# Output products, norm and routing of a one-core encoder layer, joined into one block, with hand-placed memory for the experts' weights

## The reference, cut to what matters

```python
mix = (jax.nn.sigmoid(ga) * ya + jax.nn.sigmoid(gb) * yb) @ w_out[l]
x = layer_norm(ALPHA * x + mix, ln1_g[l], ln1_b[l])
# moe_ffn(x):
scores = jax.nn.sigmoid((xt @ router_w).astype(jnp.float32))        # 512 x 64
_, sel = lax.top_k(scores + router_bias.astype(jnp.float32), TOP_K)  # 6 of 64
wsel = jnp.take_along_axis(scores, sel, axis=-1)
wsel = wsel / jnp.sum(wsel, axis=-1, keepdims=True) * ROUTED_SCALE
# each expert e, on the tokens that chose it:
gu = x_pad[tok] @ w_gate_up[e]                        # 1024 x 512
h = jax.nn.silu(gu[:, :EXPERT_DIM]) * gu[:, EXPERT_DIM:]
return (h @ w_down[e]) * wt[:, None]                  # 256 x 1024
# routed + shared expert, then the second layer_norm
```

## Time and profile before

| | us |
|---|---|
| median of 3 runs (1533.08 to 1539.72) | 1537.55 |
| the profiled execution's own time | 1532.44 |
| its span | 1530.5 |
| mean granted TensorE clock, share of full | 0.926 |

### The profile page before, as it was taken

The page is one execution under the profiler, slowest core; times in us unless marked ns, Lnnn a source line. Parts: engine busy times, 40 slices in busy tenths (PEclk is TensorE's granted clock), DMA queues, the critical chain, the costliest instruction groups (busy, mean ns, idle before and its releaser), DMA issues. The chain is left out here.

```text
span 1530.5 us, 22988 instructions
## 1 busy us (share of the span) xinstructions
PE 1309.1 (86%) x8117; PEld 772.0 (50%) x8118; DVE 444.5 (29%) x876; ACT 302.1 (20%) x817; POOL 290.5 (19%) x353
## 2 busy tenths in 40 slices
PE   6999999999998969999958789979697868978690
PEld 5465555655553438887435335534354434534340
DVE  1545544445416433332226121101010101100015
ACT  1231333223312332222030001111011101111020
POOL 2201111011107010000110222323132312322122
PEclk8999999999998989999977899989798978989795
DMA  4531111113002122334029389999999996899874
GB/s 113 155 115 48 48 41 50 49 44 137 1 1 55 28 76 80 97 96 173 14 88 373 102 305 332 335 393 392 396 371 384 392 383 223 320 374 390 330 228 170
DMA packets 134582, 294.85 MB, mean 193 GB/s; under 512 B 12928, under 2 KB 82688, under 8 KB 117968
## 3 DMA queue, kind: packets, MB, share of 16 engines
q1 hardware_dynamic: 118096, 266.77, 46.6%
q0 software_dynamic: 15552, 25.46, 7.0%
q10 hardware_dynamic: 832, 1.11, 0.2%
HBM read 278.57 MB, written 27.04 MB: 200 GB/s over the span
## 5 line engine op out<-in xcount | busy, mean ns | idle before, releaser
L1724 PE MATMUL bank<-expert_gu,gathered_xT 128*64 128x256 f32 x2048 | 254.0, 404 | 80.7 <-issue 55.5
L1724 PEld LDWEIGHTS bank<-expert_gu,gathered_xT 128*64 128x64 f32 x2048 | 166.7, 146 | 156.9 <-issue 82.9
L423 PE MATMUL bank<-xT,w_head 128*128 128x512 f32 x480 | 241.0, 613 | 1.2 <-PEq L81 1.2
L1872 DVE SCALAR_TENSOR_TENSOR hidden<-gate,slot_w,bank 128x128 f32<-128x128 f32 x64 | 22.2, 347 | 444.6 <-ACT gate L1838 433.1
L1731 PE MATMUL bank<-expert_down,hiddenT 128*64 128x512 f32 x512 | 124.0, 605 | 0.7 <-issue 0.6
L1642 POOL DMA_INDIRECT sum_rows<-expert_y,row_col x64 | 101.3, 1583 | 50.5 <-POOL row_col L1637 47.1
L423 PEld LDWEIGHTS bank<-xT,w_head 128*128 128x128 f32 x480 | 78.8, 190 | 48.5 <-issue 42.4
L1838 ACT ACTIVATE gate<-bank 128x128 f32<-128x128 f32 x64 | 17.8, 277 | 340.6 <-PE bank L1724 335.7
L601 POOL TENSOR_TENSOR LO<-LT_diagonal,level_blocks 128x256 f32<-128x256 f32 x48 | 38.2, 827 | 233.1 <-DVE LT_corner L767 233.1
L1637 POOL COPY row_col<-row_idx 128x1 int32 (+1 forms) x64 | 12.2, 191 | 304.1 <-ACT expert_y L1844 293.1
L1245 DVE TENSOR_TENSOR w_lo<-w_tile,w_hi 128x1024 fp32r<-128x1024 f32 (+1 forms) x32 | 35.5, 1112 | 116.2 <-ACT w_hi L1190 116.2
(11 more groups left out here) (325 smaller groups left out, 1873.0 us busy)
## 6 DMA issues: line engine op xcount, KB each, us to landing
expert_gu<-in_expert_w_gate_up_dram SPq DMA_DIRECT2D x128, 1024.0 KB
expert_down<-in_expert_w_down_dram SPq DMA_DIRECT2D x64, 1024.0 KB
w_head<-in_w_in_dram SPq DMA_DIRECT2D x32, 512.0 KB, 3.7
w_tile<-in_w_in_dram SPq DMA_DIRECT2D x16, 512.0 KB, 3.8
sum_rows<-zero_rows SPq DMA_DIRECT2D x2, 2048.0 KB, 11.8
w_tile<-in_w_branch_a_dram SPq DMA_DIRECT2D x8, 512.0 KB, 5.1
w_pair<-in_w_in_dram SPq DMA_DIRECT2D x6, 512.0 KB, 3.7
x_rows<-in_x_dram SPq DMA_DIRECT2D x4, 512.0 KB
```

The costliest lines, as they stand in the source:

```text
L423: mm = nc.tensor.matmul(bank[:, :], w_head[:, g, c, :], xT[:, c, :], start=(c == 0), stop=(c == KC - 1))
L1724: mm = nc.tensor.matmul(bank[parts[a], 0:2 * P], x[:, c, part], halves[:, a, :, :], start=(c == 0), stop=(c == KC - 1))
```

## The change

The phases `merge_phase` and `route_phase` become one, `mix_phase`, without the barrier between them. What it does:

- TensorE's order: the output products of tile t are interrupted by the transposes of tile t-1 (`turn_x1`) and its logits (`logits`). The transposes read `x_rows` itself with a stride of 8 elements. The shared expert's products are cut to 96 steps (32 of 128 columns, 32 of 256, 32 of 128) and dealt out by `fill(n)` where TensorE would stand.
- The norm takes two VectorE instructions per tile for scaling, gain and offset, and none on GpSimd. VectorE makes the choices of tile t-1 before it normalises tile t.
- Memory: the experts' first weights go where the split inputs (`xh`, `xl`, `dnh`, `dnl`, `w_hi`, `w_lo`, `aoh`, `aol`) lay, and are loaded as soon as the last product that reads these is made. `wo_low` goes to `dnl`, so its load waits too.
- GpSimd issues the gathers of the first four pairs at the end of `mix_phase`, after `idx_ready`; before, they stood at the head of `experts_phase`. The shared expert's down weights are loaded at the head of `experts_phase` by ScalarE's queue, and `shared_down(0)` waits for them.
- The slot of a token's rank in its expert's list changes: `spread` takes the place of `iota_e` in one comparison. Slot 16h + 4l + r holds rank 4h + l + 16((r - h) mod 4). Ranks 0 to 47 filled slots 0 to 47; now they fill three of every four adjacent slots.

```diff
-def merge_phase(nc, mem, T, ps, w_in, w_a, w_b, w_out, ln_g, ln_b, x1_rows):
+def mix_phase(nc, mem, T, ps, w_in, w_a, w_b, w_out, ln_g, ln_b, x1_rows, router_w, router_bias, ws_gu):
...
-    wo_low, wo_high = xT[:, :, :].rearrange("p (c a) n -> p c (a n)", a=2), T["bias"][:, :, :].rearrange("p (c a) n -> p c (a n)", a=2)
+    wo_low, wo_high = (at(f"w_out_{n}", [P, KC // 2, D], n) for n in ("dnl", "bias"))
...
+    x_cols = [T["av"][:, 2 * t:2 * t + 2, :].rearrange("p a n -> p (a n)") for t in range(2)]
...
-            for c, part in ((0, wo_low), (KC // 2, wo_high)):
-                sp.dma_start(part, w_out[c * P:(c + KC // 2) * P, :].rearrange("(c p) n -> p c n", p=P)).then_inc(wo_in, 16)
+            load_out(wo_high, KC // 2)
             sp.wait_ge(ao_split, 1)
...
-            for t in range(TT):
-                sp.wait_ge(permuted[t], 1)
-                sp.dma_start(x1_rows[t * P:(t + 1) * P, :], x_cols[t]).then_inc(x1_out, 16)
-            sp.wait_ge(x1_out, 16 * TT)
+            sp.dma_start(wr[:, :, :], router_w.rearrange("(p c) n -> p c n", p=P)).then_inc(r_in, 16)
+            sp.dma_start(brow[:, :], router_bias.partition_broadcast(P)).then_inc(r_in, 16)
+            sp.wait_ge(prod[1][1], TURNS)
+            load_out(wo_low, 0)
+            T["load_gu"](sp, 2, 2)
+            sp.wait_ge(prod[1][2], TURNS)
+            T["load_gu"](sp, 0, 0)
+            T["load_gu"](sp, 1, 1)
+            sp.wait_ge(prod[1][3], TURNS)
+            for s in range(GROUP):
+                T["load_down"](sp, s, s)
+            sp.dma_start(wg[:, :, :], ws_gu.rearrange("(p c) n -> p c n", p=P)).then_inc(s_in, 16)
+            for t in range(TT - 1):
+                x1_rows_out(t)
+            sp.wait_ge(mix_psum[TT - 1], 1)
+            T["load_gu"](sp, 3, 3)
+            x1_rows_out(TT - 1)
...
+            def mix(t, half, cs):
+                for c in cs:
+                    mm = nc.tensor.matmul(ps[2 * t + half][:, :], mT[:, c, tile(t)], wo(c)[:, half * HALF:(half + 1) * HALF],
+                                          start=(c == 0), stop=(c == KC - 1))
+                return mm
+            def turn_x1(t):
+                pe.wait_ge(ln_done[t], 1)
+                columns = xs[:, t, :].rearrange("p (q c) -> p c q", c=KC)
+                for half in range(2):
+                    for c in range(KC // 2):
+                        mm = nc.tensor.transpose(ps[2 * t + half][:, tile(c)], columns[:, half * KC // 2 + c, :], ident[:, :])
+                    mm.then_inc(x1t_psum[t], 1)
+            def logits(t):
+                pe.wait_ge(x1t_ready[t], 2)
+                for c in range(KC):
+                    mm = nc.tensor.matmul(ps[2 * t][:, 0:NE], xT[:, c, tile(t)], wr[:, c, :], start=(c == 0), stop=(c == KC - 1))
+                mm.then_inc(lg_psum[t], 1)
+            def shared_steps():
+                for lo, hi in ((0, P), (P, 3 * P), (3 * P, SEQ)):
+                    for g in range(4):
+                        for c in range(KC):
+                            mm = nc.tensor.matmul(shared_bank[g][:, lo:hi], wg[:, c, tile(g)], xT[:, c, lo:hi],
+                                                  start=(c == 0), stop=(c == KC - 1))
+                            if hi == SEQ and c == KC - 1:
+                                mm.then_inc(sg_psum[g], 1)
+                            yield
...
             pe.wait_ge(wo_in, 32)
             for p in range(2):
                 pe.wait_ge(merged[p], TURNS)
+            pe.wait_ge(r_in, 32)
             for t in range(TT):
-                for half in range(2):
-                    for c in range(KC):
-                        mm = nc.tensor.matmul(ps[2 * t + half][:, :], mT[:, c, t * P:(t + 1) * P],
-                                              wo(c)[:, half * HALF:(half + 1) * HALF], start=(c == 0), stop=(c == KC - 1))
-                mm.then_inc(mix_psum[t], 1)
-            for c in range(KC):
-                for t in range(TT):
-                    if c == 0:
-                        pe.wait_ge(permuted[t], 1)
-                    if c >= 4:
-                        pe.wait_ge(x1t_ready, c - 3)
-                    mm = nc.tensor.transpose(ps[c % 4][:, t * P:(t + 1) * P], x_cols[t][:, c * P:(c + 1) * P], ident[:, :])
-                mm.then_inc(x1t_psum, 1)
+                mix(t, 0, range(KC))
+                if t:
+                    turn_x1(t - 1)
+                mm = mix(t, 1, range(KC // 2))
+                if t:
+                    logits(t - 1)
+                mix(t, 1, range(KC // 2, KC)).then_inc(mix_psum[t], 1)
+            pe.wait_ge(s_in, 16)
+            pe.wait_ge(sc_done[0], 1)
+            fill(32)
+            turn_x1(TT - 1)
+            fill(3)
+            logits(TT - 1)
+            fill(6)
...
+            fill(23)
+            for part in range(PARTS):
+                pe.wait_ge(lists_ready[part], 1)
...
+                if part < PARTS - 1:
+                    fill(4)
+            mm.then_inc(list_psum, 1)
+            fill(3)
...
+            fill(96)
...
+            for p in range(2):
+                act.wait_ge(merged[p], TURNS)
             for t in range(TT):
+                nc.scalar.preload_act_table_set(LN_EXP)
                 act.wait_ge(ag_done[t], 1)
...
-                if t:
-                    permute(t - 1)
+                nc.scalar.preload_act_table_set(SIGMOID)
+                if t < TT - 1:
+                    permute(t)
+                for half in range(2 if t < TT - 1 else 1):
+                    copy_x1(t, half)
+                act.wait_ge(lg_psum[t], 1)
+                nc.scalar.activation(score[:, t, :], ps[2 * t][:, 0:NE], ACT.Sigmoid).then_inc(sc_done[t], 1)
             permute(TT - 1)
-            for c in range(KC):
-                act.wait_ge(x1t_psum, c + 1)
-                nc.scalar.copy(xT[:, c, :], ps[c % 4][:, :]).then_inc(x1t_ready, 1)
+            nc.scalar.preload_act_table_set(SILU)
+            for k in range(2):
+                act.wait_ge(sg_psum[k], 1)
+                nc.scalar.activation(hT[:, k, :], shared_bank[k][:, :], ACT.Silu).then_inc(sg_act[k], 1)
+                if k == 0:
+                    act.wait_ge(slot_psum, 1)
+                    nc.scalar.copy(T["slot_w"][:, :], ps[6][:, 0:LISTS])
...
-            pool.wait_ge(ln_in, 32)
-            for t in range(TT):
-                pool.wait_ge(ln_m[t], 1)
-                nc.gpsimd.tensor_tensor(xs[:, t, :], xs[:, t, :], b_row, ALU.add).then_inc(ln_done[t], 1)
...
+            for h in range(4):
+                of_h = spread[:, 16 * h:16 * h + 16].rearrange("p (l r) -> p l r", r=4)
+                for r0, r1, first in ((h, 4, 0), (0, h, 16 * (4 - h))):
+                    if r0 < r1:
+                        nc.gpsimd.iota(of_h[:, :, r0:r1], pattern=[[1, 4], [16, r1 - r0]], base=4 * h + first,
+                                       channel_multiplier=0, allow_small_or_imprecise_dtypes=True).then_inc(gs, 1)
...
+            for k in range(2):
+                pool.wait_ge(x1_out[k], 32)
+            pool.wait_ge(idx_ready, 1)
+            for q in range(GROUP):
+                nc.gpsimd.tensor_copy(T["col"][:, q:q + 1], T["tok_idx"][:, q:q + 1]).then_inc(first_col[q], 1)
+                pool.wait_ge(first_col[q], 1)
+                nc.gpsimd.indirect_dma_start(
+                    out=T["xg"][:, q, :], out_offset=None, in_=x1_rows[:, :],
+                    in_offset=bass.IndirectOffsetOnAxis(ap=T["col"][:, q:q + 1], axis=0),
+                    bounds_check=last_token, oob_is_err=False).then_inc(T["gathered"][q], 16)
...
+                dve.wait_ge(ag_done[t], 1)
+                nc.vector.scalar_tensor_tensor(out=xs[:, t, :], in0=xs[:, t, :], scalar=mv[:, t, 0:1], in1=g_row,
+                                               op0=ALU.subtract, op1=ALU.mult).then_inc(ln_m[t], 1)
+                dve.wait_ge(ln_m[t], 1)
                 dve.wait_ge(ln_rs[t], 1)
-                nc.vector.tensor_scalar(xs[:, t, :], xs[:, t, :], mv[:, t, 0:1], mv[:, t, 3:4],
-                                        ALU.subtract, ALU.mult).then_inc(ln_n[t], 1)
-                dve.wait_ge(ln_n[t], 1)
-                nc.vector.tensor_tensor(xs[:, t, :], xs[:, t, :], g_row, ALU.mult).then_inc(ln_m[t], 1)
...
+                nc.vector.scalar_tensor_tensor(out=xs[:, t, :], in0=xs[:, t, :], scalar=mv[:, t, 3:4], in1=b_row,
+                                               op0=ALU.mult, op1=ALU.add).then_inc(ln_done[t], 1)
+            def choose(t):
+                dve.wait_ge(sc_done[t], 1)
+                then(nc.vector.tensor_tensor(biased[:, t % 2, :], score[:, t, :], brow[:, :], ALU.add))
+                then(nc.vector.max(top[:, t, :], biased[:, t % 2, :]))
+                then(nc.vector.max_index(topi[:, t, :], top[:, t, :], biased[:, t % 2, :]))
+                then(nc.vector.tensor_copy(topf[:, t, :], topi[:, t, :]))
+                one = [P, TOPK, NE]
```

(27 more changed lines are left out.)

428 lines of the change are left out of this document (194 added, 234 removed).

## The result

The changed kernel takes 1497.12 us (median of 4 runs, 1495.94 to 1501.05), the kernel before 1538.63 on the same chip. The ratio is 0.9722, with a 95% interval of 0.9697 to 0.9746. The series of the first experiments gave 0.9721. The forecast was 1485, with a range of 1460 to 1508: the sign and the range held, and the median lies 12 us above the forecast. The profiled execution took 1497.2 us, with a span of 1495.5 and a clock of 0.936.

A forecast was written before the change was run, and what follows sets the result against it. Bound by a dependent chain from the last output product to the first expert, then by the weight stream. Span 1530.5 - 34.2 (front) - 18 (slots) = 1478.3, with 1.9 and 5.1 added 1485.4 us; range 1460 to 1508.

The forecast's parts named there:

- The front: Output products to the first expert's transpose: first transpose at 834.0 instead of 868.20, 34.2 us earlier.
- From `count` to the first expert: Indices, gathers and barrier ahead of the first expert: gathers start at 824.5, barrier costs 1.17 us, gain 11.8 us.
- `wo_low` and the down weights at nothing: Later loads for output products and shared expert: late by 0 to 2.5 and up to 3.5 us, both taken as 0.
- The interleaving is free: Transposes and logits between tiles' output products: no wait between, the next half tile's 6.9 us covers the 5.6 us norm.
- The slots: Long stretch of experts, 960 to 1478: new slot order evens gathers and scatters over DMA engines, 18 us saved.
- 28 us are saved from a stream that waits for the slowest: Long stretch: if empty slots fall on few engines, the others carry 111 us against a mean of 83; upper bound.
- The two short windows of the earlier trace: DMA at 0.71 in the 4 us to 1260, read as uneven engines; at 0.17 in 4 us at 1448, as running dry.
- the stretch of 610 us: First expert to last weights, 868 to 1478: if it stays at 610 us, the slots did nothing.
- nothing from the slots: Rival for the long stretch: the order of slots changes nothing, 1503 us; chance 0.24.
- More than its share: Rival for the long stretch: waits for the slowest engine also starve DMA, 42 us gained there, 1461 us; chance 0.12.
- The light engines were the slow ones: Rival: engines with the empty slots set each load's end and now get 28 us more, 1531 us; chance 0.06.
- Rows did not get dearer: Rival: adjacent slots holding ranks 16 apart make each row dearer, 1545 us at 50% dearer; chance 0.03.

The follow-up runs named there:

- the first experiments: First series of follow-up runs, which ran the unchanged changed kernel again against the kernel before: 1494.09 us, ratio 0.9721.
- slots_plain: Changed kernel with the slots filled in the order of before (0, 1, 2): 1504.63 us, ratio 0.9785 to the kernel before.
- not_interleaved: Changed kernel with all four tiles' output products in one piece, the first three tiles' transposes and logits behind them: 1514.99 us, ratio 0.9842.
- uneven orders: Changed kernel with slots in plain order, reversed, or one pair of groups of four always full (two mirrored runs): 1504.63, 1509.02, 1512.31 and 1510.33 us.
- small_weights: Changed kernel reloading one of four chunks of the second half of gate and up for experts after the first four: 1466.11 us, ratio 0.9517.
- before_spread: Kernel before with only the new order of slots: 1529.55 us, ratio 0.9945.
- the mirrored orders: Changed kernel with slots 28 to 31 and 60 to 63 always full, or 0 to 3 and 32 to 35: 1512.31 and 1510.33 us.

## Why the prediction was right, and where its terms were off

- **The front, 34.2 us predicted, 33.6 in the profile, 33.3 by the time of `slots_plain`.** The sum was right, its terms less so: the 2.5 us that it had too little ahead of `count` and the 3.0 too much behind it cancel, which is luck. To `count` the gain is 24.9 and not 22.4. The transposes take 0.88 us a tile and not 1.7: with a stride of 8 elements each is one record of 0.11 us. I had read a pair of records in the earlier trace rows as one transpose, and it was two. The logits take 1.73 as predicted. The last tile's chain was about right.
- **From `count` to the first expert, 11.8 predicted, 8.8 measured** (41.4 before, 32.65 after). The four gathers occupy GpSimd for 6.6 us (823.99 to 830.61) and not 8.35, but the barrier took 5.93 and not "1.17 as before". The step that failed here is that the barrier "waits for all four gathers to be issued"; it ended only after their rows had landed. The early gathers by themselves are worth 3.6, and the other 5.2 come from what was moved besides them.
- **`wo_low` and the down weights at nothing:** right. The first output product has the same wait of 1.70 us as before (1.60), and no wait for `ws_down` appears.
- **The interleaving is free:** right, and `not_interleaved` shows what it avoids: 15 us in the front, half of it by the clock and the rest mostly waits for copies.
- **The slots, 18 us predicted, 8.4 and 10.5 measured.** The direction and the mechanism held (uneven orders cost 10 to 14 us, by the waits for loads), and the size was off. The step that failed is "28 us are saved from a stream that waits for the slowest". By the earlier trace rows all engines together were busy for 0.96 of 518 us, so a fullest engine could be at most 21 us above the mean, not 28. And TensorE waited for loads for 34.4 us in all; with next to no such waits the stretch was still 484 us, in `small_weights`. The two short windows of the earlier trace rows were a sample of two and could not tell how often such a moment comes; the table of waits would have. The prediction's own sign was whether the stretch of 610 us stays. In the profiles it is 607.5 (836.5 to 1444), which settles nothing, as the profiled run of before lay 5 us under its median; the medians of `slots_plain` and `before_spread` settle it.
- **The rivals:** "nothing from the slots" (1503) lies 6 us from the median and so nearer to it than the forecast, 12. By the result alone it could not be told from a half-sized gain; `slots_plain` and `before_spread` refute it. "More than its share" (1461) misses. "The light engines were the slow ones" (1531) falls, since the even order made both kernels faster; that an engine is slower by less is left open by the mirrored orders. Rows did not get dearer: q0 has the same share, 16.2% against 16.1%.

18 less some 9.5 is 8.5 us of the 12 by which the median exceeds the forecast; the rest is within the spread of the runs (1495.94 to 1501.05).

## What to carry to other kernels

Where DMA is at 0.96 and the matrix engine still works for four fifths of the time, add up that engine's waits for transfers over the stretch, before any estimate per DMA engine, as the first bound on a gain on the transfers. It is not the whole: `small_weights` gained 32 us in a stretch with 26.7 of such waits, the rest by a higher clock. A barrier behind indirect gathers costs the gathers' whole latency; with only the first of them ahead of it, the front here was 5.5 us shorter. Small dependent products go between large independent ones: the same transposes and logits cost 8.0 us between the output products and 21.5 behind them.
